# A two-block model on one core: the order of the first stage's sums, tables, folds and slabs

## The chip, the core and the metric

The kernel runs on one core of a Trainium2 chip. All work is float32. The metric is the device time of one execution in microseconds; the profile adds one profiled execution, with the time of every instruction. Engines: TensorE (PE; its weight loads are PEld), VectorE (DVE), ScalarE (ACT), GpSimd (POOL), and SyncE (SP), which here only issues transfers.

## What is computed

A token model with 512 tokens of width 1024 (`x`) and 256 context tokens (`ctx`), in two blocks of two layers each. The change touches only the beginning of the first layer of the first block:

```python
def adaln_params(cvec, w, b):
    return jnp.split(jax.nn.silu(cvec) @ w + b, 6, axis=-1)

def fourier_mix(h, w_o, b_o):
    bsz, t, _ = h.shape
    hg = h.astype(jnp.float32).reshape(bsz, t, FNET_GROUPS, FNET_GROUP_DIM)
    f = jnp.fft.fft2(hg, axes=(1, 3), norm='ortho').real
    return f.reshape(bsz, t, D_MODEL).astype(h.dtype) @ w_o + b_o

# layer 0 of first_block
sh1x, sc1x, g1x, sh2x, sc2x, g2x = adaln_params(c, ada_w[i], ada_b[i])
hx = rmsnorm(x, norm_g[i, 0]) * (1.0 + sc1x) + sh1x
x = x + g1x * fourier_mix(hx, fnet_wo[fi], fnet_bo[fi])      # the same for ctx with c_ctx
hx = rmsnorm(x, norm_g[i, 1]) * (1.0 + sc2x) + sh2x
x = x + g2x * ec_moe(hx, moe_router[i], moe_wg[i], moe_wu[i], moe_wd[i])
```

Then follow a second layer with a recurrent mixer and another expert stage, and a second block of two attention layers with feed-forward parts. None of that is touched.

## The kernel before

Everything is laid out with channels on the 128 partitions: `resx` is x as 8 tiles (KT = 8) of 128 x 512, `resc` the context as 8 tiles of 128 x 256. Weights come as slabs of 128 x 4096 float32 (2 MB), one transfer each, into a ring of three places; slab n goes to place n modulo 3, in the order of the list `FRONT`: a0 to a3, w0, w1, a4 to a11, tables. The slabs a0 to a11 are `ada_w` of the layer, w0 and w1 are the output weights of the Fourier mixer, and "tables" holds cosines and sines that are fetched in two pieces into `work` (`load_tables`: first C and S, 514 columns, later the other 2690). `vecs` are all small vectors, `tabs1` constant matrices of 2338 columns whose first 128 are the identity `ident` and whose next 128 are `ones`.

There is no scheduler. Each engine's program is written out by hand in the order in which it runs, and semaphores join them. An engine waits in its own order, so whatever stands behind a waiting instruction waits too. `Steps` and `Side` only count semaphore values. SP issues transfers in order as well, each behind its own wait: slab n may be loaded when slab n - 3 has been used, which PE reports (`slab_used`) for the a slabs, and GpSimd (`norm_pool`) for w0 and w1.

The front, in order:

- **Sums of squares.** ACT computes silu(c) into `cs`, changes its function table, and squares the 8 tiles of x into `sqx0`. DVE squares the context (`sqc0`), adds its halves (step "context"), then adds the halves of x's squares (steps "added"). PE sums over the partitions by multiplying with `ones`: first the context, then x (step "sums"). ACT makes 1/root of it (`rstd`).
- **Folding of tokens.** DVE multiplies x and the context by `rstd` (`ux`, `uc`) and adds and subtracts mirrored tokens into `hx` and `hc` (step "folded"), since a cosine needs only the even part and a sine the odd part.
- **Modulation 0.** PE multiplies silu(c) with a0 to a3 (`ada_slab`), ACT copies the sums, PE transposes them with `ident` (`ada_turned(0)`) and then runs some matmuls whose results nobody reads (`kept_warm`). DVE makes scale and shift of them (`modulation(0)`).
- **Scaling.** ACT scales and shifts the 8 tiles of `hx` (L2247, L2248), two instructions a tile; DVE does the same for the 8 tiles of `hc` (L2846, L2847), and counts each in `norm_dve`.
- **First phase** (channels): PE multiplies `hx` and `hc` with C and S, twice 7 tiles, the seventh being the two Nyquist columns `nyq`. DVE copies each result out of PSUM (L2856). PE uses six banks and waits for a copy before it uses a bank again.
- **GpSimd's folds.** Behind step "folded" GpSimd adds and subtracts the halves of w0 and of w1 into `wsum` (L3696, L3697, four instructions of 128 x 2048), and copies 4 rows of the tables (L3700). The third phase reads `wsum`.
- **Second phase** (tokens): PE multiplies with the cosines and sines of tokens, 9 results, copied by DVE (L2865, L2867). Before them DVE clears a small table (memset, L2859).
- **Modulation 1**: a4 to a7, copy, transposes. ACT then adds a bias to resx and resc, PE makes a shift for the router.
- **Third phase** (output weights): for f = 0 to 7, two results each; ahead of f = 0 to 3 stand a8 to a11. DVE adds the results to resx and resc.
- **Routing and experts.** PE, DVE and ACT choose tokens for 16 experts; GpSimd gathers the rows of the first two with indirect transfers (`gathered`). PE runs `kept_warm(P[1], 8)` before it transposes them and goes through 96 expert slabs.

Of the kernel before, what the change touches and what calls it, by code (L numbers as in the profile page):

```python
# [29 lines left out]
KT = D // 128  # L30
NX, NC = 512, 256
# [29 lines left out]
TAB1 = {}  # L61
# [6 lines left out]
NTAB1 = _n  # L68
# [12 lines left out]
FN = {}  # L81
# [212 lines left out]
AD_DVE = [("context",)] + [("added", _k) for _k in range(4)] + [("folded",)] + [("mod", _g) for _g in range(3)]  # L294
# [111 lines left out]
def build(nc, slabs_d, vecs_d, tabs1_d, tabs2_d, aux_d, lora_d, x_d, ctx_d, out_d, kv_d):  # L406
# [5 lines left out]
    with stack:  # L412
# [3 lines left out]
        def sem(name):  # L416
            return stack.enter_context(nc.semaphore(name))
# [31 lines left out]
        ad_pe, ad_dve, ad_act, x_loaded, context_loaded, waves_loaded = (sem(n) for n in ("ad_pe", "ad_dve", "ad_act", "x_loaded", "context_loaded", "waves_loaded"))  # L449
        rt_pe, rt_dve, rt_act, places_loaded = (sem(n) for n in ("rt_pe", "rt_dve", "rt_act", "places_loaded"))  # L450
# [49 lines left out]
        adarow = [work[:, at:at + HALF] for at in (KT * HALF, KT * HALF + HALF, 2 * KT * HALF - HALF)]  # L500
        cs = cut(work, WORK - 2 * KT - KT * 32, KT, 32)
# [368 lines left out]
        def _(sp):  # L870
            sp.dma_start(resx[:, :, :], x_d.rearrange("(k p) t -> p k t", p=128)).then_inc(x_loaded, 16)
            sp.dma_start(vecs[:, :], vecs_d).then_inc(tables_loaded, 16)
            sp.dma_start(resc[:, :, :], ctx_d.rearrange("(k p) t -> p k t", p=128)).then_inc(context_loaded, 16)
            sp.dma_start(tabs1[:, :], tabs1_d[:, 0:NTAB1]).then_inc(tables_loaded, 16)
# [4 lines left out]

            load_tables(0, FN["S"][1])  # L880
# [54 lines left out]
            used = 0  # L935
            for n in range(RING, f0):
                before = FRONT[n - RING]
                if before in ("w0", "w1"):
                    sp.wait_ge(norm_pool, 1 + int(before[1]))
                else:  # L940
                    used += 1
                    sp.wait_ge(slab_used, used)
                if FRONT[n] == "tables":
                    sp.dma_start(ring[n % RING][:, 0, 0:4], slabs_d[n][:, 0:4]).then_inc(slab_loaded[n % RING], 16)
                else:
                    load(n)
                if FRONT[n] == "a3":
                    load_tables(FN["S"][1], FN["w128"][1])
# [68 lines left out]
        def _(pe):  # L1017
# [79 lines left out]
            pe.wait_ge(tables_loaded, 32)  # L1097
# [40 lines left out]

            pe.wait_ge(*ad_done("dve", "context"))
            for k in range(4):  # L1140
                mm(P[5][:, 0:NC], ones, sqc0[:, k, :], k, 4)
            for k in range(4):
                pe.wait_ge(*ad_done("dve", "added", k))
                m = mm(P[4][:, :], ones, sqx0[:, k, :], k, 4)
# [4 lines left out]
            pe.wait_ge(fed, me.next("fed"))  # L1149
            for n in range(4):  # L1150
                ada_slab(n)
            ada_turned(0)
            kept_warm(P[0], 4)
# [10 lines left out]
            for pair in range(2):  # L1164
                for i, (src, at, n, part, _) in enumerate(FN_TILES):
                    if me.reuses():

                        pe.wait_ge(drained, me.reused())
                    b = me.next_bank()
                    name, wide_ = ("S", 128) if part is AO else ("C", 129)  # L1170
                    for q in range(2):
                        for k in range(2):
                            kt = 4 * pair + 2 * q + k
                            if i == 0:
                                shifted(kt)
                            if i == 4:
                                scaled(kt)
                            m = mm(b[0:n, wide_ * q:wide_ * (q + 1)], src[:, kt, at:at + n], fn(name, k, wide_), k, 2)
                    m.then_inc(filled, me.add("filled"))
            pe.wait_ge(fed, me.next("fed"))  # L1180
# [27 lines left out]
            me.t["slab"].n += 2  # L1208
            for n in range(4, 8):
                ada_slab(n)  # L1210
# [57 lines left out]
            def first_routing():  # L1268
# [57 lines left out]
                kept_warm(P[1], 8)  # L1326
# [860 lines left out]
        def _(act):  # L2187
# [35 lines left out]
            act.wait_ge(tables_loaded, 32)  # L2223
# [10 lines left out]

            act.wait_ge(x_loaded, 16)
            for k in range(4):
                for half in range(2):
                    tile_square(k + 4 * half, [(resx, sqx0)], wait=False)
            act.wait_ge(*ad_done("pe", "sums"))
# [515 lines left out]
        def _(v):  # L2755
# [41 lines left out]
            v.memset(tiny, 1e-6)  # L2797
            v.drain().then_inc(fed, me.add("fed"))
            t["answered"].n += 1
            ad = Steps(AD_DVE)  # L2800
            v.wait_ge(context_loaded, 16)
# [3 lines left out]
            for k in range(4):  # L2805
                v.wait_ge(norm_act, 2 * k + 2)
                v.tensor_tensor(sqx0[:, k, :], sqx0[:, k, :], sqx0[:, k + 4, :], ALU.add).then_inc(ad_dve, ad.one("added", k))
# [15 lines left out]
            def modulation(g):  # L2823

                v.wait_ge(*ad_done("pe", "turned", g))
                v.wait_ge(tables_loaded, 32)
# [628 lines left out]
            with me.loop("layer", 2) as l:  # L3455
# [91 lines left out]
                v.wait_ge(tables_loaded, 48)  # L3547
# [140 lines left out]
        def _(pool):  # L3688
            me = Side(pool, K)
            pool.wait_ge(norm_act, KT + 1)  # L3690
            pool.wait_ge(*ad_done("dve", "folded"))
# [401 lines left out]
```

## Time and profile before

| what | value |
|---|---|
| median of three runs | 3798.23 us (3795.86 to 3805.44) |
| the profiled execution | 3813.2 us, its span 3811.4 us |
| mean granted TensorE clock | 0.987 of full |
| PE busy over the span | 3615.1 us, 95% |
| first phase, copies included | about 45 to 75.5 us of the span |
| second phase | 75.5 to 92 us |
| third phase | 110.7 to 170 us |
| routing | 171 to 215 us |
| first expert stage | 215 to 800 us |

Times in the rows count from the start of the span. A matmul of float32 stands in the trace as two records, so 32 records of 128 x 129 are 16 matmuls; a slab of `ada_w` is 32 matmuls and 64 records. A timeline row merges neighbours of a kind, with their count (x) and the time from the first one's start to the last one's end. The brackets give the idle time of the engine before the row and what ended it. An engine that is not the bound may idle without harm; what counts is PE's idle time.

### The profile page before, as it was taken

The page shows a single profiled execution, that of the slowest core. Times are in us where ns is not written, and L with a number is a line of the kernel's source. Part 1 is how long each engine was busy: PE and PEld are TensorE (multiplying, and loading weights), DVE is VectorE, ACT ScalarE, POOL GpSimd, SP SyncE. Part 2 cuts the span into 40 slices and gives each one's busy share as a digit, 9 for nine tenths or more (in the row PEclk, how much of TensorE's full clock was granted, in tenths as well). Part 3 has the DMA queues.
Part 4 walks back from the last instruction along what each step waited for, and adds up shares of the span by engine and source line. Part 5 has one row for each costly group of instructions (what it writes and reads, how often), then busy time and mean ns, then how long its engine had stood idle before and what let it go on. Part 6 is the DMA issues. An engine that isn't in the chain of part 4 may idle for free.

```text
span 3811.4 us, 84045 instructions
## 1 busy us (share of the span) xinstructions
PE 3615.1 (95%) x35378; PEld 2256.1 (59%) x35378; DVE 1599.2 (42%) x3423; ACT 802.1 (21%) x1802; POOL 704.3 (18%) x634
## 2 busy tenths in 40 slices
PE   6999999989989899899999999989999999999998
PEld 4544444455567777764444344455888744658887
DVE  5321111164566666643212133742445437425454
ACT  1210010020145565541000011070000010610000
POOL 2100001000044444420000000002343300023433
PEclk8999999999999999999999999999999999999999
DMA  6699999942200000022999981101222211012221
GB/s 267 266 394 383 383 378 374 390 189 86 92 12 14 18 18 13 14 82 113 427 429 428 428 338 45 67 24 64 83 78 86 98 45 67 24 48 86 88 89 45
DMA packets 56774, 626.04 MB, mean 164 GB/s; under 512 B 6080, under 2 KB 9408, under 8 KB 20928
## 3 DMA queue, kind: packets, MB, share of 16 engines
q1 hardware_dynamic: 50096, 599.22, 39.2%
q0 software_dynamic: 3968, 14.16, 1.3%
q10 hardware_dynamic: 2448, 8.91, 0.6%
q8 instruction: 195, 3.19, 0.3%
q14 instruction: 67, 0.55, 0.0%
HBM read 604.18 MB, written 18.09 MB: 163 GB/s over the span
## 4 chain that ended last, share of the span: by engine, by line
PE 85%; DVE 6%; DMA 3%; issue 2%; ACT 2%; DVEq 1%; ACTq 1%; PEld 0%; PEldq 0%; SPq 0%
PE bank L1022 69%; PE bank L1588 11%; DMA work<-slabs 2%; PE bank L1970 1%; PE bank L1983 1%; PE bank L1643 1%; PE bank L1050 1%; DVE hx L2788 1%; DVE work L2764 1%; ACT work L2667 1%; ACTq L2668 1%; DMA ring<-slabs 1%; PEld bank L1022 0%; DVE work L2773 0%; PE bank L1451 0%
## 5 line engine op out<-in xcount | busy, mean ns | idle before, releaser
L1022 PE MATMUL bank<-work 128*64 128x512 f32 (+11 forms) x5232 | 874.8, 424 | 29.6 <-DVE work L2856 13.9
L1022 PEld LDWEIGHTS bank<-work 128*128 128x128 f32 (+6 forms) x5232 | 504.4, 153 | 369.2 <-issue 273.6
L1022 PE MATMUL bank<-ring,work 128*32 128x256 f32 (+2 forms) x4416 | 472.2, 429 | 21.8 <-DMA ring<-slabs 14.2
L1022 PE MATMUL bank<-hx,ring 128*128 128x512 f32 (+1 forms) x1344 | 483.3, 514 | 5.1 <-DVE hx L2788 2.8
L1022 PE MATMUL bank<-work,ring 128*128 128x256 f32 (+1 forms) x1616 | 479.7, 455 | 6.5 <-DVE work L3150 3.4
L1022 PEld LDWEIGHTS bank<-work,ring 128*128 128x128 f32 x1616 | 306.2, 190 | 173.5 <-issue 131.7
L1022 PEld LDWEIGHTS bank<-hx,ring 128*128 128x128 f32 x1344 | 254.3, 191 | 222.0 <-issue 200.7
L1022 PEld LDWEIGHTS bank<-ring,work 128*32 128x32 f32 (+1 forms) x4416 | 193.0, 122 | 287.0 <-issue 242.8
L3835 POOL TENSOR_TENSOR work<-ring 128x512 f32<-128x512 f32 (+1 forms) x44 | 69.4, 1577 | 1564.5 <-ACT work L2196 1167.4
L2764 DVE TENSOR_TENSOR work<-work,bank 128x256 f32<-128x256 f32 x240 | 91.8, 416 | 384.6 <-ACT work L2742 380.3
L1588 PE MATMUL bank<-work 64*64 64x64 f32 x9216 | 196.8, 228 | 28.3 <-issue 17.0
L1022 PE MATMUL bank<-hx,work 128*32 128x256 f32 (+3 forms) x1344 | 211.4, 416 | 1.1 <-issue 1.0
L1588 PEld LDWEIGHTS bank<-work 64*64 64x64 f32 x9216 | 177.8, 139 | 39.2 <-issue 37.3
L1022 PEld LDWEIGHTS bank<-hx,work 128*32 128x32 f32 (+2 forms) x1344 | 131.9, 145 | 63.1 <-issue 40.2
L2742 ACT ACTIVATE work<-bank 128x256 f32<-128x256 f32 x48 | 18.5, 385 | 693.8 <-PE bank L1022 693.8
L1588 PE MATMUL bank<-ring,work 64*64 64x128 f32 (+2 forms) x2912 | 152.5, 287 | 5.8 <-DVE hx L3260 3.1
L3053 DVE TENSOR_TENSOR work<-work,bank 128x256 f32<-128x256 f32 x16 | 6.8, 423 | 325.7 <-PE bank L1022 325.7
L3640 DVE SCALAR_TENSOR_TENSOR work<-work 128x256 f32<-128x256 f32 x176 | 122.9, 713 | 15.5 <-issue 6.0
L1022 PE MATMUL bank<-resc,work 128*128 128x256 f32 x512 | 121.2, 379 | 0.6 <-DVE resc L3628 0.6
L1588 PEld LDWEIGHTS bank<-ring,work 64*64 64x64 f32 x2912 | 106.5, 133 | 15.2 <-issue 14.1
L3054 DVE TENSOR_TENSOR work<-work,bank 128x512 f32<-128x512 f32 x32 | 21.9, 685 | 208.3 <-PE bank L1022 208.3
L3188 DVE TENSOR_TENSOR work<-bank,tabs_sb 128x384 f32<-128x384 f32 x160 | 87.9, 555 | 44.3 <-PE bank L1588 41.9
(391 smaller groups left out, 4538.0 us busy)
## 6 DMA issues: line engine op xcount, KB each, us to landing
ring<-slabs SPq DMA_DIRECT2D x176, 2048.0 KB, 10.6
work<-slabs SPq DMA_DIRECT2D x82, 2048.0 KB, 15.9
hx<-slabs SPq DMA_DIRECT2D x17, 2048.0 KB, 12.0
work<-kv SPq DMA_DIRECT2D x18, 384.0 KB, 3.1
kv<-work SPq DMA_DIRECT2D x2, 3072.0 KB, 15.9
kv<-work ACTq DMA_DIRECT2D x6, 512.0 KB, 5.3
resx<-xT SPq DMA_DIRECT2D x1, 2048.0 KB, 8.4
kv<-work POOLq DMA_DIRECT2D x1, 2048.0 KB, 29.6
```

The lines of the kernel that those rows point to most:

```text
L1022: return pe.matmul(out, lhsT, rhs, start=(k == 0), stop=(k == n - 1))
L1050: pe.matmul(b[:, 0:width], ident, tabs1[:, 0:width], start=True, stop=True)
L1588: m = pe.matmul(out[other if across else r], lhsT[r], rhs[r], start=first, stop=last)
L1643: pe.matmul(outw[:, 0:n], wa2[two[d], 0:128], HW[two[d], at:at + n], start=True, stop=True)
L1970: m = pe.matmul(out[:, 0:n], q[rows_of(h), 128 * i:128 * i + 128], key[rows_of(h), k0:k1], start=(part == 0), stop=(part == parts - 1 and ...
L1983: m = pe.transpose(out[:, a:a + 128], S[:, h, a:a + 128], ident)
L2667: act.activation(S[:, h, 0:n], at_bank("L", u, h)[:, 0:n], ACT.Exp, bias=low, scale=-1.0, accum_out=sums[u % 2][:, h:h + 1])
L2668: act.drain().then_inc(at_act, ak.one("exp", u, h))
L2764: v.tensor_tensor(out, a, b, op)
L3188: v.tensor_tensor(by_halves(TL, g), level_banks("H", g), bc(levels[:, 1 - d, l, :].unsqueeze(1).unsqueeze(1), 128, 2, 3, CH), ALU.mult).th ...
L3640: return v.scalar_tensor_tensor(dst, x, 1.0, y, ALU.mult, ALU.subtract)
L3835: pool.tensor_tensor(s3, a["a11"], a["a21"], ALU.subtract).then_inc(ff_pool, 1)
```

## The change

1. SP fetches only the first 128 columns of `tabs1` (the identity) ahead of a0. The other 2210 columns and the rest of the sine tables are issued behind a3, the first piece of the sine tables behind a2. `vecs`, the identity and the rest of tabs1 get semaphores of their own. PE waits for the identity before the transposes, and for the rest of tabs1 before `kept_warm`; `modulation` on DVE waits for vecs and for the rest of tabs1.
2. ACT loads its silu table at once, squares x as soon as x has landed, and computes silu(c) behind the squares. DVE adds the halves of x's squares first and squares the context behind them. PE sums x first and the context second, with a block of ones that DVE has written itself (`early_ones`), so that it doesn't wait for tabs1.
3. GpSimd's folds wait for the eighth count of `norm_dve`, which is DVE's last scaling of the context, in place of step "folded".
4. PE takes slab a4 between the first and the second phase; a5 to a7 stay behind the second.
5. `kept_warm` runs 3 matmuls for 4 behind the transposes, and 5 for 8 before the experts.

```diff
-AD_DVE = [("context",)] + [("added", _k) for _k in range(4)] + [("folded",)] + [("mod", _g) for _g in range(3)]
+AD_DVE = [("added", _k) for _k in range(4)] + [("context",), ("folded",)] + [("mod", _g) for _g in range(3)]
...
+        early_ones = adarow[2][:, 0:128]
...
-            sp.dma_start(vecs[:, :], vecs_d).then_inc(tables_loaded, 16)
+            sp.dma_start(vecs[:, :], vecs_d).then_inc(vectors_loaded, 16)
             sp.dma_start(resc[:, :, :], ctx_d.rearrange("(k p) t -> p k t", p=128)).then_inc(context_loaded, 16)
-            sp.dma_start(tabs1[:, :], tabs1_d[:, 0:NTAB1]).then_inc(tables_loaded, 16)
+            first = TAB1["ident"][1]
+            sp.dma_start(tabs1[:, 0:first], tabs1_d[:, 0:first]).then_inc(identity_loaded, 16)
...
-            load_tables(0, FN["S"][1])
...
+            load_tables(0, FN["S"][1])
             for n in range(RING, f0):
...
                 if FRONT[n] == "a3":
+                    sp.dma_start(tabs1[:, first:NTAB1], tabs1_d[:, first:NTAB1]).then_inc(tables_loaded, 16)
                     load_tables(FN["S"][1], FN["w128"][1])
...
-            pe.wait_ge(tables_loaded, 32)
...
+            pe.wait_ge(fed, me.next("fed"))
+            for k in range(4):
+                pe.wait_ge(*ad_done("dve", "added", k))
+                mm(P[4][:, :], early_ones, sqx0[:, k, :], k, 4)
             pe.wait_ge(*ad_done("dve", "context"))
             for k in range(4):
-                mm(P[5][:, 0:NC], ones, sqc0[:, k, :], k, 4)
-            for k in range(4):
-                pe.wait_ge(*ad_done("dve", "added", k))
-                m = mm(P[4][:, :], ones, sqx0[:, k, :], k, 4)
+                m = mm(P[5][:, 0:NC], early_ones, sqc0[:, k, :], k, 4)
...
             for n in range(4):
                 ada_slab(n)
+            pe.wait_ge(identity_loaded, 16)
             ada_turned(0)
-            kept_warm(P[0], 4)
+            pe.wait_ge(tables_loaded, 16)
+            kept_warm(P[0], 3)
...
+            me.t["slab"].n += 2
+            ada_slab(4)
             pe.wait_ge(fed, me.next("fed"))
             pe.wait_ge(waves_loaded, 32)
...
-            me.t["slab"].n += 2
-            for n in range(4, 8):
+            for n in range(5, 8):
                 ada_slab(n)
...
-                kept_warm(P[1], 8)
+                kept_warm(P[1], 5)
...
+            act.preload_act_table_set("silu_and_others")
+            act.wait_ge(x_loaded, 16)
+            for k in range(4):
+                for half in range(2):
+                    tile_square(k + 4 * half, [(resx, sqx0)], wait=False)
+            act.wait_ge(vectors_loaded, 16)
             act.wait_ge(fed, 1)
...
             v.memset(tiny, 1e-6)
+            v.memset(early_ones, 1.0)
...
-                v.wait_ge(tables_loaded, 32)
+                v.wait_ge(vectors_loaded, 16)
+                v.wait_ge(tables_loaded, 16)
...
             pool.wait_ge(norm_act, KT + 1)
-            pool.wait_ge(*ad_done("dve", "folded"))
+            pool.wait_ge(norm_dve, KT)
```

Where the instructions stand. PE at the end of the first phase, before (`work 2x129` are the Nyquist columns, `work 128x257` the first result of the second phase):

```order
L1022 MATMUL bank<-work,hc 127x128 x4
L1022 MATMUL bank<-work 2x129 x4
L1022 MATMUL bank<-work 128x257 x3
L1022 MATMUL bank<-work 128x129 x2
L1022 MATMUL bank<-work 128x255 x2
L1022 MATMUL bank<-work 128x127
```

and now:

```order
L1025 MATMUL bank<-work,hc 127x128 x4
L1025 MATMUL bank<-work 2x129 x4
L1025 MATMUL bank<-ring,work 32x128 x32
L1025 MATMUL bank<-work 128x257 x3
L1025 MATMUL bank<-work 128x129 x2
L1025 MATMUL bank<-work 128x255 x2
L1025 MATMUL bank<-work 128x127
```

The 32 matmuls out of the ring, slab a4, have moved between the phases; behind the second one 96 are left of 128.

SP at the program's start, before (`tabs_sb` is tabs1, `work<-slabs` the sine tables):

```order
L871 DMA resx<-xT 128x8x512
L872 DMA vecs_sb<-vecs 128x607
L873 DMA resc<-ctxT 128x8x256
L874 DMA tabs_sb<-tabs 128x2338
L878 DMA work<-slabs 128x514
L884 DMA ring<-slabs 128x4096 x4
L878 DMA work<-slabs 128x2690
L884 DMA ring<-slabs 128x4096 x10
```

and now:

```order
L873 DMA resx<-xT 128x8x512
L874 DMA vecs_sb<-vecs 128x607
L875 DMA resc<-ctxT 128x8x256
L877 DMA tabs_sb<-tabs 128x128
L885 DMA ring<-slabs 128x4096 x3
L881 DMA work<-slabs 128x514
L885 DMA ring<-slabs 128x4096
L950 DMA tabs_sb<-tabs 128x2210
L881 DMA work<-slabs 128x2690
L885 DMA ring<-slabs 128x4096 x10
```

Most of tabs1 has moved behind a3, and stands ahead of w0 like the rest of the sine tables.

GpSimd's folds, with the semaphores that each waits for, before:

```order
L3696 TENSOR_TENSOR work<-ring 128x2048 [waits slab_loaded1,ad_dve,norm_act]
L3697 TENSOR_TENSOR work<-ring 128x2048
L3696 TENSOR_TENSOR work<-ring 128x2048 [waits slab_loaded2]
L3697 TENSOR_TENSOR work<-ring 128x2048
L3700 COPY work<-work 4x1024 [waits waves_loaded]
```

and now:

```order
L3704 TENSOR_TENSOR work<-ring 128x2048 [waits slab_loaded1,norm_dve,norm_act]
L3705 TENSOR_TENSOR work<-ring 128x2048
L3704 TENSOR_TENSOR work<-ring 128x2048 [waits slab_loaded2]
L3705 TENSOR_TENSOR work<-ring 128x2048
L3708 COPY work<-work 4x1024 [waits waves_loaded]
```

The order is the same; the first fold's wait for a step of DVE (`ad_dve`) has become one for DVE's scaling (`norm_dve`).

## Rows read from the trace of the kernel before

**Rows 1.** The page's first line, the whole program.

```profile
span 3811.4 us, 84045 instructions
```

**Rows 2.** Windows: length, busy us (instructions) by engine, PE clock, DMA share, GB/s.

```profile
core 0: us, PE busy (x) PEld busy (x) DVE busy (x) ACT busy (x) POOL busy (x), PEclk, DMA share, GB/s
0.00:45.00 45.00, 22.23 (x283) 15.73 (x284) 22.57 (x30) 11.35 (x20) 0.20 (x4) 0.89 0.96 392
45.00:75.00 30.00, 15.66 (x114) 13.28 (x113) 25.34 (x25) 5.43 (x13) 19.37 (x5) 0.77 0.64 253
75.00:110.00 35.00, 27.95 (x402) 20.91 (x406) 6.49 (x15) 2.44 (x5) 0.00 (x0) 0.95 0.43 176
215.00:800.00 585.00, 581.32 (x5234) 246.17 (x5236) 91.62 (x225) 56.68 (x146) 39.41 (x54) 1.00 0.94 369
...
31.00:42.00 11.00, 7.65 (x130) 6.30 (x131) 9.36 (x9) 0.60 (x1) 0.00 (x0) 0.53 1.01 426
```

**Rows 3.** Timeline, 37 to 50 us: start, us, engine, line, operation, [idle <-releaser].

```profile
37.28 3.64 PE L1022 MATMUL bank<-ring,work 128*32 128x128 f32 x64 [1.09 <-DMA ring<-slabs]
...
42.25 3.60 PE L1050 MATMUL bank<-tabs_sb 128*128 128x512 f32 x8
42.45 0.19 DVE L2764 TENSOR_TENSOR mod<-bank,vecs_sb 128x32 f32<-128x32 f32 x1 [2.02 <-PE bank L1117]
...
46.92 3.16 PE L1022 MATMUL bank<-work,hx 128*128 128x129 f32 x26 [0.40 <-ACT hx L2248]
```

**Rows 4.** DMA issues of the first 8 us: KB each, median us to landing.

```profile
tabs_sb<-tabs SPq DMA_DIRECT2D x1, 1169.0 KB, 13.4
```

**Rows 5.** Timeline, the first phase, 44 to 75 us.

```profile
44.05 0.35 DVE L2846 TENSOR_SCALAR hc<-hc,work,mod 128x128 f32<-128x128 f32 x1
...
44.50 0.34 DVE L2846 TENSOR_SCALAR hc<-hc,work,mod 128x128 f32<-128x128 f32 x1
...
45.55 4.67 POOL L3696 TENSOR_TENSOR work<-ring 128x2048 f32<-128x2048 f32 x1 [45.08 <-DMA ring<-slabs]
45.66 4.64 DVE L2847 TENSOR_SCALAR hc<-hc,work 128x127 f32<-128x127 f32 x1
...
65.29 2.07 DVE L2856 COPY work<-bank 128x258 f32<-128x258 f32 x6
...
65.75 1.88 PE L1022 MATMUL bank<-work 128*2 128x129 f32 x8 [13.89 <-DVE work L2856]
...
67.56 4.63 PE L1022 MATMUL bank<-work,hx 128*128 128x129 f32 x32
...
73.90 1.05 PE L1022 MATMUL bank<-work 128*2 128x129 f32 x8
```

**Rows 6.** Timeline, 1082 to 1083.6 us, in the second layer: DVE beside GpSimd.

```profile
1082.30 0.64 POOL L3802 TENSOR_TENSOR work<-work,tabs_sb 128x256 f32<-128x256 f32 x1 [19.61 <-ACT work L2396]
...
1082.77 0.41 DVE L3260 COPY hx<-bank 128x256 f32<-128x256 f32 x1
```

**Rows 7.** Timeline, PE from 75 to 119 us.

```profile
75.54 16.50 PE L1022 MATMUL bank<-work 2*128 2x257 f32 x73 [0.60 <-DVEq L2857]
...
102.90 3.24 PE L1022 MATMUL bank<-ring,work 128*32 128x128 f32 x64 [4.86 <-DMA ring<-slabs]
...
108.57 0.31 PE L1022 MATMUL bank<-ring,work 128*32 128x128 f32 x3
...
117.06 1.96 PE L1022 MATMUL bank<-ring,work 128*32 128x128 f32 x64
```

**Rows 8.** DMA issues at 54.8 us (a5), 64.1 (a6) and 94.0 (a7).

```profile
ring<-slabs SPq DMA_DIRECT2D x1, 2048.0 KB, 7.6
...
ring<-slabs SPq DMA_DIRECT2D x1, 2048.0 KB, 8.4
...
ring<-slabs SPq DMA_DIRECT2D x1, 2048.0 KB, 8.9
```

**Rows 9.** Timeline, 206 to 215 us: PE's warming matmuls, SP behind `gathered`.

```profile
206.76 10.02 PE L1050 MATMUL bank<-tabs_sb 128*128 128x512 f32 x16
...
214.38 0.33 SPq L894 DMA_DIRECT2D hx<-slabs  x1
```

More of the change, by code:

```diff
@@ L449, in build @@
         ad_pe, ad_dve, ad_act, x_loaded, context_loaded, waves_loaded = (sem(n) for n in ("ad_pe", "ad_dve", "ad_act", "x_loaded", "context_loaded", "waves_loaded"))
+        vectors_loaded, identity_loaded = sem("vectors_loaded"), sem("identity_loaded")
         rt_pe, rt_dve, rt_act, places_loaded = (sem(n) for n in ("rt_pe", "rt_dve", "rt_act", "places_loaded"))
@@ L1148, in _ @@
             pe.wait_ge(answered, 1)
-            pe.wait_ge(fed, me.next("fed"))
             for n in range(4):
                 ada_slab(n)
+            pe.wait_ge(identity_loaded, 16)
             ada_turned(0)
-            kept_warm(P[0], 4)
+            pe.wait_ge(tables_loaded, 16)
+            kept_warm(P[0], 3)
             me.first_bank()
@@ L2222, in _, with ada_copied @@
             both = [(resx, sqx), (resc, sqc)]
-            act.wait_ge(tables_loaded, 32)
+            ad = Steps(AD_ACT)
+            def ada_copied(g):
+                act.wait_ge(*ad_done("pe", "summed", g))
+                act.activation(adarow[g], P[7][:, :], ACT.Copy).then_inc(ad_act, ad.one("copied", g))
+            act.preload_act_table_set("silu_and_others")
[4 more added lines that the diff above has]
+            act.wait_ge(vectors_loaded, 16)
             act.wait_ge(fed, 1)
@@ L2227, in _ @@
             act.preload_act_table_set("natural_log_exp_and_others")
-            ad = Steps(AD_ACT)
-            def ada_copied(g):
-                act.wait_ge(*ad_done("pe", "summed", g))
-                act.activation(adarow[g], P[7][:, :], ACT.Copy).then_inc(ad_act, ad.one("copied", g))
[L2235 to L2238, printed above, removed]
             act.wait_ge(*ad_done("pe", "sums"))
@@ L2800, in _ @@
             ad = Steps(AD_DVE)
+            for k in range(4):
+                v.wait_ge(norm_act, 2 * k + 2)
+                v.tensor_tensor(sqx0[:, k, :], sqx0[:, k, :], sqx0[:, k + 4, :], ALU.add).then_inc(ad_dve, ad.one("added", k))
             v.wait_ge(context_loaded, 16)
@@ L2804, in _ @@
             v.tensor_tensor(sqc0[:, 0:4, :], sqc0[:, 0:4, :], sqc0[:, 4:8, :], ALU.add).then_inc(ad_dve, ad.one("context"))
-            for k in range(4):
-                v.wait_ge(norm_act, 2 * k + 2)
-                v.tensor_tensor(sqx0[:, k, :], sqx0[:, k, :], sqx0[:, k + 4, :], ALU.add).then_inc(ad_dve, ad.one("added", k))
             v.wait_ge(norm_act, KT + 1)
@@ L3546, in _ @@
                 scaled(segs, rstd2, lambda k, j: pv[:, k:k + 1])
-                v.wait_ge(tables_loaded, 48)
+                v.wait_ge(tables_loaded, 32)
                 taken("cqi0", ("x", "cqi0"))
```

## The prediction

> **What bounds the kernel now.** I read the page first: one core, span 3811.4 us [rows 1]. Everything that the diff moves lies before 217 us. The table of windows [rows 2] says where TensorE (PE) is not the bound: it is busy 22.2 of the first 45 us, 15.7 of the 30 us from 45 to 75, 28.0 of the 35 from 75 to 110, but 581.3 of the 585 us of the expert stage. So time can be won in the first 110 us, and what is won there should stay won, because PE, not a transfer, fills what follows.
>
> The timeline then names the wait that ends last in each piece. To 41 us it is the stream of transfers: slab a3 starts on PE at 37.28, when it has landed, and takes 3.64 us, about twice the 1.96 of a slab at full clock [rows 3, 7]. Behind it come its copy, the transposes, VectorE's (DVE) `mod(0)` at 42.45 and ScalarE's scaling; PE goes on in earnest at 46.92, released by ScalarE's fourth tile [rows 3]. The worst piece is 45 to 66 us [rows 5]: GpSimd starts to fold w0 at 45.55, in instructions of 4.67 us, and DVE's context scaling, whose pairs had started 0.45 us apart, now has instructions of 4.64. Only behind the sixteenth, at 65.29, do DVE's copies out of PSUM (L2856) start, and PE has waited 13.89 us for the first. The last piece is a7: its ring place is free only when a4 is used, which stands behind the second phase, and PE waits 4.86 us more at 102.90 [rows 7].
>
> **Step 1, tables fetched later.** tabs1 is 1169 KB ahead of a0 [rows 4]; 64 KB of it (the identity) stay. The 1105 KB that leave are 1.13 MB: at 392 to 426 GB/s [rows 2] that is 2.9 to 2.7 us. a3 lands 2.7 us sooner, as long as it is issued (after a0 is used) before the stream runs dry, which step 2 makes safer. Its consumers follow: `mod(0)` at 39.8, ScalarE's fourth tile at 44.2 for 46.92. The rest of tabs1 is now behind a3 and lands 2.7 us after it, at about 37.3; `mod(0)` and the warming matmuls, which now wait for it, are reached at 39.5 or later, so 2 us cover that wait; without them both would start late by what is missing. w0 and a4 stand behind the same bytes as before. **Gain 2.7.**
>
> **Step 2, squares when x lands, sums of x before those of context.** The sums end several us sooner. But PE then waits for a1, a2 and a3 as before, and DVE's products only end earlier ahead of a `mod(0)` that they did not delay: DVE had been idle for 2.02 us before it, waiting for PE's transposes [rows 3]. Worth 0, hidden by a3's landing; it would cost only if a0 were used later than today.
>
> **Step 3, three warming matmuls for four (L1050).** Four end at 45.85 under the wait for 46.92 [rows 3]; three end at about 42.3 under 44.2. Worth 0, unless the clock falls in the 2 us behind them (below).
>
> **Step 4, GpSimd behind DVE's scaling.** With `mod(0)` at 39.8, scaling starts near 41 and its eight pairs at 0.45 us end at 44.6. w0 lands at 45.4 as now, so GpSimd starts at the same 45.5 and ends its four folds (4.6 us each) at the same 64.1: its chain costs nothing new. DVE goes on to the PSUM copies. The price hangs on one question: does a copy out of PSUM also stand still under a GpSimd instruction? The nearest rows are at 1082 us [rows 6]: a 128x256 copy out of PSUM starts 0.47 us into a GpSimd tensor_tensor of 0.64 us and takes 0.41 us. So I take no blocking. The 13.89 us go, and with them the half clock that the gap brought: the 8 Nyquist records took 1.88 us behind it and 1.05 later, and the 32 records behind them 4.63 where 26 at full clock took 3.16 [rows 3, 5]; that is 0.8 + 0.7. The first phase ends at 73.90 + 1.05 - 2.7 - 13.9 - 1.5 = 56.8. **Gain 15.4.** Late next is nothing on DVE: its memset (L2859) may stand under GpSimd for up to 4.6 us, but PE has six banks free there, over 10 us of work.
> The Trainium skill, SBUF — State Buffer, sections "SBUF: two separate sides" and "Who interferes with whom", says that VectorE and GpSimd take a common port pair exclusively, for a whole instruction, and lists copies among VectorE's that do; taken alone it puts L2856 under the lock (the third rival). VectorE: DVE Perf Modes, section "Mode 2×_2P", restricts the two-port form to SBUF operands; by that L2856 is free. The scaling under GpSimd (4.64 us) agrees with the first, the copy at 1082.77 (0.41 us) with the second.
>
> **Step 5, slab a4 between the phases.** From w0's 45.4, a4 lands two slabs of 2.1 MB later, 4.9 us each at 426 GB/s, at 55.2. At 56.8 PE takes it without a wait: 1.96 us and 0.1 to hand over [rows 7]. It covers the 0.6 us in which PE waited for DVE's last copy. The second phase starts at 58.9 for 75.54 and, taking 16.5, ends at 75.4. SP's loads stand in order: a5 behind GpSimd's first fold, a6 behind the second, a7 behind a6. a6 takes 8.4 us from 64.1 [rows 8], a7 one slab more: 77.4. PE reaches a7 at 75.4 + 2 x 2.05 = 79.5 and ends it at 81.5, for 102.90 + 3.24 = 106.14 now. So here 24.6 us are won: 2.7, 15.4, 0.6 and, of a7, the wait of 4.86 and 1.3 of half clock, less roundings.
> The new wait is a8. It is loaded when a5 is used, now at 77.5; a load alone takes 7.6 to 8.9 us [rows 8], so it lands at 85.1 to 86.4. PE is there at 84.0 (2.43 us behind a7's end, as 108.57 is now [rows 7]). Cost 1.1 to 2.4, I take 1.8. If the clock is then at half, a8 takes 3.6 for 1.96: of 0 to 1.7 I take 0.5. **Net 22.3** at the third phase's start. a9 to a11 have over 6 us of PE work between them, and the stream needs 4.9 a slab.
>
> **Step 6, five warming matmuls for eight ahead of the experts.** Eight (16 records) took 10.02 us from 206.76 [rows 9]; at full clock, where 8 records take 3.60 [rows 3], they take 7.2, so some six or seven ran at half. The gathered rows were there at 214.4, where SP's wait for them ends [rows 9], yet PE was in matmuls until 216.8. Five would have ended near 214.3, and at full clock eight end at 214.0 and nothing is won. So 0 to 2.3; I take 1.2.
>
> **Sum.** 22.3 + 1.2 = 23.5 us. The profiled execution took 3813.2 (span 3811.4), so a like one would take 3789.7; the median of the three runs is 15 us under it, and 3798.2 - 23.5 = 3774.7, 0.62% less. About 0.3% (11.4 us) is what a measurement of this kernel tells from no change; its three runs spread over 9.6.
>
> **Rivals.**
> *The clock or small waits eat part.* The front still has idle pieces (behind a1, up to 44.2, before a8), and the granted clock was 0.53 from 31 to 42 and 0.77 from 45 to 75 [rows 2]. If one more stretch of 10 us of PE work runs at half, the gain is 13.5: 3784.7. For it: less warming. Against: after the long gap PE was back at full clock within some 4 us of work.
> *Nothing arrives, because the expert stage ends on its transfers.* They are busy 0.94 there. Against: PE is busy 0.994, and the loads hang on steps that all move. It would give about 3796.
> *The copies stand under GpSimd after all* (the change does not do what it says). Then one gets through per GpSimd instruction until 65.3, 9 of 14 remain, the first phase ends near 70 (gain 5), and a4's new place still removes the wait for a7, less a8's: 10 to 11 us, 3787.5. Against it: [rows 6].
> *Slower.* With three warming matmuls and sparse work from 42.3 to 44.2 the clock falls to half as PE enters the first phase and stays there through both: 12.8 + 16.5 = 29 us of work doubled against 23.5 won, 3803.7. It decides from 23.5 us of work at half. Against: the clock was 0.95 from 75 to 110 with PE busy 28 of 35 us [rows 2].
>
> **How the numbers follow.** Forecast 0.70; clock or small waits 0.13; copies blocked 0.06; nothing arrives 0.07; slower 0.04. Range: at best 24.6 - 1.1 + 2.3 = 25.8, and 3.4 more if a2 and a3 ran at full clock, gives 3769; with the runs' spread 3767. Upwards it takes in the first and third rival, 3788. Faster by over 0.3%: 0.70 + 0.13 + a part of copies blocked, less a little for the spread, 0.84; within 0.3%: 0.12; slower: 0.04.
>
> **What would show it.** Right: DVE's 16 scalings at about 0.3 us each and over before GpSimd starts; copies (L2856's) of 0.43 us under its 4.6; the wait of 13.9 gone; a4 at 57 without a wait; a new wait of 1 to 2.5 us for a8 near 84; the third phase 22 us sooner, the expert stage 22 to 25. Wrong: copies of over 1 us under GpSimd; `mod(0)` waiting for the tables near 40; a granted clock of one half in either phase; an expert stage longer than its 585 us.

## The result

| | before | the changed kernel |
|---|---|---|
| median of the runs of one measurement | 3813.61 us (3795.86 to 3819.13, 11 runs) | 3791.74 us (3787.61 to 3794.96, 11 runs) |
| ratio | | 0.995, 95% interval 0.9936 to 0.9964 |
| profiled execution, its span | 3813.2, 3811.4 us | 3789.2, 3787.4 us |

The change is faster by 13.7 to 24.4 us. The two profiled executions differ by 24.0 us, and the prediction's sum of gains was 23.5; the match is closer than it earned, since 2.6 us of the 24.0 arise in a part that nothing changed (below). Yet the predicted time, 3774.7 with a range of 3767 to 3788, lies 17 us under the measured one, which is outside the range. The sum was taken off the median of three runs, 3798.2; more runs of the same kernel give 3813.6. Why the median of three runs of the kernel before could lie 15 us under that of eleven is the main thing that the experiments had to settle.

### The profile page after: what moved, and what is told of

Its sections match the earlier page's. It is cut to its first block, busy times and chain, and to the rows that moved or that the text cites. A ratio compares the mean times of both kernels' runs of the same rounds, so it can differ in the third digit from the quotient of the medians.

```text
span 3787.4 us, 84032 instructions
## 1 busy us (share of the span) xinstructions
PE 3608.6 (95%) x35370; PEld 2250.7 (59%) x35370; DVE 1582.7 (42%) x3424; ACT 802.6 (21%) x1802; POOL 703.2 (19%) x634
## 4 chain that ended last, share of the span: by engine, by line
PE 84%; DVE 5%; DMA 3%; issue 2%; ACT 2%; DVEq 1%; PEld 1%; ACTq 1%; PEldq 0%; POOL 0%; POOLq 0%; SPq 0%
PE bank L1025 68%; PE bank L1593 12%; DMA work<-slabs 2%; PE bank L1975 1%; PE bank L1988 1%; PE bank L1648 1%; PEld bank L1025 1%; DVE hx L2794 1%; DMA ring<-slabs 1%; DVE work L2770 0%; ACT work L2673 0%; ACTq L2674 0%; DVE work L2779 0%; DVE work L3217 0%; PE bank L1456 0%
## 5 line engine op out<-in xcount | busy, mean ns | idle before, releaser
L1025 PE MATMUL bank<-work 128*32 128x256 f32 (+11 forms) x5248 | 882.3, 425 | 27.6 <-DVE work L2810 11.2
L1025 PEld LDWEIGHTS bank<-work 128*128 128x128 f32 (+4 forms) x5248 | 508.3, 153 | 370.6 <-issue 287.2
L3648 DVE SCALAR_TENSOR_TENSOR work<-work 128x256 f32<-128x256 f32 x176 | 123.4, 716 | 15.4 <-issue 6.1
## 6 DMA issues: line engine op xcount, KB each, us to landing
work<-slabs SPq DMA_DIRECT2D x82, 2048.0 KB, 15.7
kv<-work SPq DMA_DIRECT2D x2, 3072.0 KB, 15.7
```

What stands on the lines that cost most here:

```text
L1025: return pe.matmul(out, lhsT, rhs, start=(k == 0), stop=(k == n - 1))
L3648: return v.scalar_tensor_tensor(dst, x, 1.0, y, ALU.mult, ALU.subtract)
```

## The profile after

The page's first line, answering [rows 1]:

```profile
span 3787.4 us, 84032 instructions
```

The windows of the changed kernel (length, busy us and instructions by engine, PE clock, DMA share, GB/s), answering [rows 2]:

```profile
31.00:42.00 11.00, 8.26 (x110) 5.87 (x103) 6.34 (x17) 1.91 (x4) 0.00 (x0) 0.65 1.01 425
45.00:75.00 30.00, 29.72 (x240) 23.18 (x238) 10.81 (x23) 2.91 (x7) 19.04 (x5) 1.00 0.80 316
45.00:90.00 45.00, 41.03 (x519) 32.69 (x518) 11.96 (x28) 9.91 (x21) 19.04 (x5) 0.96 0.81 321
200.00:800.00 600.00, 591.24 (x5427) 253.94 (x5424) 105.22 (x251) 67.44 (x163) 39.42 (x54) 0.99 0.94 370
```

From 45 to 75 us PE is now busy for 29.7 of the 30 us, where before it had been busy for 15.7 of them [rows 2]. To 42 us the granted clock is still low, 0.65.

The timeline of the changed kernel, 34 to 60 us (start, us, engine, line, operation, in brackets the idle time before it and what ended it), answering [rows 3] and [rows 5]:

```profile
34.83 3.64 PE L1025 MATMUL bank<-ring,work 128*32 128x128 f32 x64 [1.94 <-DMA ring<-slabs]
...
39.94 0.19 DVE L2770 TENSOR_TENSOR mod<-bank,vecs_sb 128x32 f32<-128x32 f32 x1 [4.25 <-PE bank L1119]
...
44.49 0.28 DVE L2855 TENSOR_SCALAR hc<-hc,work 128x127 f32<-128x127 f32 x1
...
45.73 4.53 POOL L3704 TENSOR_TENSOR work<-ring 128x2048 f32<-128x2048 f32 x1 [45.26 <-DMA ring<-slabs]
45.82 0.43 DVE L2864 COPY work<-bank 128x258 f32<-128x258 f32 x1 [0.47 <-PE bank L1025]
...
54.92 4.53 POOL L3704 TENSOR_TENSOR work<-ring 128x2048 f32<-128x2048 f32 x1 [0.18 <-issue]
...
56.59 1.99 PE L1025 MATMUL bank<-ring,work 128*32 128x128 f32 x61
...
57.58 0.48 DVE L2867 MEMSET work<- 128x512 f32 x1 [0.29 <-issue]
...
58.87 16.50 PE L1025 MATMUL bank<-work 2*128 2x257 f32 x73 [0.28 <-issue]
```

Slab a3 starts 2.45 us sooner and still takes 3.64 us. DVE's last context scaling ends at 44.77 (44.49 + 0.28), 1.0 us ahead of GpSimd's first fold, and the fold was released by w0's landing, not by DVE: its new wait costs nothing. The copies out of PSUM (L2864) take 0.43 us while a fold of 4.53 runs, and so does the memset: 0.48 us at 57.58, inside the fold that ends at 59.45 (54.92 + 4.53). The wait of 13.89 us is gone, a4 follows the first phase without a wait, and the second phase starts at 58.87 for 75.54 [rows 7].

The same view further on, answering [rows 7] and [rows 9]: the new wait for a8, the third phase, and the stretch ahead of the experts.

```profile
86.10 3.39 PE L1025 MATMUL bank<-ring,work 128*32 128x128 f32 x64 [1.89 <-DMA ring<-slabs]
...
89.58 6.58 PE L1025 MATMUL bank<-work 128*128 128x386 f32 x18
...
184.73 6.57 PE L1053 MATMUL bank<-tabs_sb 128*128 128x512 f32 x10
192.14 1.09 PE L1400 MATMUL bank<-tabs_sb,work 128*128 128x128 f32 x8 [0.84 <-DMA work<-kv,index]
...
196.47 19.09 PE L1025 MATMUL bank<-ring,work 128*64 128x512 f32 x144 [2.58 <-ACT work L2329]
215.37 5.50 PE L1025 MATMUL bank<-hx,work 128*32 128x256 f32 x48
```

And the kernel before at the same three points:

```profile
110.66 6.47 PE L1022 MATMUL bank<-work 128*128 128x386 f32 x18
...
216.62 1.04 PE L1395 MATMUL bank<-tabs_sb,work 128*128 128x128 f32 x8
...
220.88 16.13 PE L1022 MATMUL bank<-ring,work 128*64 128x512 f32 x144 [2.58 <-ACT work L2323]
236.82 5.49 PE L1022 MATMUL bank<-hx,work 128*32 128x256 f32 x48
```

The distance between the two is 21.1 us at the third phase, 24.5 at the transposes of the gathered tokens (216.62 to 192.14), and 21.45 behind the first 144 expert records (236.82 to 215.37), since these now take 19.09 for 16.13 us. The other 2.6 us of the 24.0 arise later, where nothing was changed. That part, from the start of the experts' next stage (215.37 and 236.82) to the end of the span, takes 3567.0 to 3575.7 us over the thirteen profiled executions of this study (3574.6 before, 3572.0 in the changed kernel), so 2.6 us of it are scatter.

## The experiments

The ratios are to the kernel before, which ran on the same chip beside them; its runs are told of in a paragraph of their own below. Steps are numbered as in the prediction.

**fold_early: step 4 undone, all else kept.**

```
-            pool.wait_ge(norm_dve, KT)
+            pool.wait_ge(*ad_done("dve", "folded"))
```

> The changed kernel with one line of it undone: GpSimd's folds wait for step folded again, not for VectorE's context scaling. Theory A (tables and fold are each enough): with tabs1 behind a3 the sixteen scalings end at 44.8 us of the span and w0 lands at 45.3, so the fold starts at 45.7 whatever it waits for, the scalings stay at 0.3 us, and the time is that of the changed kernel within 2 us. Theory B (the prediction's step 4, the fold's new wait brings the 13.9 us): scalings of 4.6 us under the fold, VectorE's PSUM copies from 65 us, 14 to 18 us slower than the changed kernel.

Measured: 3788.86 us (3782.34 to 3794.69, 10 runs), ratio 0.9949 (0.9935 to 0.9964). Its timeline has the last scaling at 44.63 and the fold at 45.87:

```profile
44.63 0.28 DVE L2855 TENSOR_SCALAR hc<-hc,work 128x127 f32<-128x127 f32 x1
...
45.87 4.53 POOL L3704 TENSOR_TENSOR work<-ring 128x2048 f32<-128x2048 f32 x1 [45.41 <-DMA ring<-slabs]
```

GpSimd was allowed to go first and did not, because w0 had not landed. With the tables out of the way, the new wait is not needed: the prediction gave it the whole credit for the 13.9 us.

**tables_first: step 1 undone, step 4 kept** (the rest of tabs1 is issued right behind the identity).

```
             sp.dma_start(tabs1[:, 0:first], tabs1_d[:, 0:first]).then_inc(identity_loaded, 16)
+            sp.dma_start(tabs1[:, first:NTAB1], tabs1_d[:, first:NTAB1]).then_inc(tables_loaded, 16)
...
-                    sp.dma_start(tabs1[:, first:NTAB1], tabs1_d[:, first:NTAB1]).then_inc(tables_loaded, 16)
```

> The changed kernel with all of tabs1 fetched ahead of a0 again (identity and rest right behind each other); the fold's new wait stays. Theory A and B alike: mod(0) 2.6 us later, near 42.5, scalings near 43.6 to 47.2 at 0.3 us each, GpSimd's first fold at 47.3 in place of 45.7, second phase 2.6 us later than the changed kernel's 58.87, the whole 2 to 3 us slower than the changed kernel. If the tables were worth nothing: 0.

Measured: 3793.43 us (3786.76 to 3800.56, 12 runs), ratio 0.9965 (0.9947 to 0.9982). Now GpSimd does wait for DVE, and no scaling is stretched:

```profile
46.90 0.29 DVE L2855 TENSOR_SCALAR hc<-hc,work 128x127 f32<-128x127 f32 x1
...
47.33 4.54 POOL L3704 TENSOR_TENSOR work<-ring 128x2048 f32<-128x2048 f32 x1 [46.87 <-DVE hc L2855]
...
91.94 6.89 PE L1025 MATMUL bank<-work 128*128 128x386 f32 x18
```

The third phase starts 2.4 us later than in the changed kernel, which is the price of the tables at that point. Steps 1 and 4 each remove the stall without the other.

**both_back: both undone** (the two edits above together).

> The changed kernel with both of these undone: all of tabs1 ahead of a0, and GpSimd's folds behind step folded. Theory A: w0 lands at 45.4 with only four pairs scaled, the port block is back, scalings of 4.6 us until 65.3, a PE wait of 13 to 14 us for the first PSUM copy, second phase at 77 for 58.87 and the whole 17 to 19 us slower than the changed kernel. Rival (the order of squares and sums gave part of the gain): less than 15.

Measured: 3806.76 us (3785.94 to 3815.44, 12 runs), ratio 0.9996 (0.9979 to 1.0012). Two runs took 3785.94 and 3794.14, the ten others 3802.39 to 3815.44. The profiled execution is the fastest of them, and shows no stall:

```profile
37.34 1.95 PE L1025 MATMUL bank<-ring,work 128*32 128x128 f32 x64 [1.90 <-DMA ring<-slabs]
...
40.77 0.19 DVE L2770 TENSOR_TENSOR mod<-bank,vecs_sb 128x32 f32<-128x32 f32 x1 [5.05 <-PE bank L1119]
...
45.32 0.28 DVE L2855 TENSOR_SCALAR hc<-hc,work 128x127 f32<-128x127 f32 x1
...
45.59 4.54 POOL L3704 TENSOR_TENSOR work<-ring 128x2048 f32<-128x2048 f32 x1 [45.12 <-DMA ring<-slabs]
```

This was the experiment that changed the theory. If its two groups of times are the stall and its absence, the same kernel runs with the stall and without it: it is a **race**, in which either DVE's last scaling or GpSimd's first fold comes first. Here a3 ran at full clock (1.95 us), the sixteen scalings end at 45.60, and GpSimd, released by w0's landing, starts at 45.59, just too late to stretch one. If a3 takes 3.64, `mod(0)` comes at 42.4 [rows 3] and the scalings, undisturbed, need until 47.2 (46.90 + 0.29 in fold_only below, where a3 takes 3.64 too), so GpSimd gets in between. The next two runs force the race either way.

**both_back_warm: the race decided by the clock.** In both_back, PE is kept busy with spare matmuls while it waits for a2 and a3:

```
             for n in range(4):
+                for _ in range((0, 0, 4, 2)[n]):
+                    pe.matmul(P[0][:, :], early_ones, resx[:, 0, :], start=True, stop=True)
                 ada_slab(n)
```

> The kernel with tabs1 first and the folds behind step folded (runs from 3786 to 3815), plus 4 matmuls without use ahead of a2 and 2 ahead of a3, where PE waits for transfers. Theory R with the clock as what decides: a3 then runs at full clock (1.96 us for 3.64), mod(0) comes at 40.8 for 42.4, the scaling ends at 45.6 as the fold starts, and wins or loses one instruction of 4.6 us: median 3788 to 3795, few runs above 3800. Rival (the clock has nothing to do with it): the same two clusters, median near 3807.

Measured: 3791.38 us (3787.59 to 3793.37, 6 runs), ratio 0.9954 (0.994 to 0.9967). All six are as fast as the changed kernel, and none is in the group above 3802. The window from 31 to 42 us has a granted clock of 1.00 (that is 2.4 GHz), where it was 0.53 before [rows 2]:

```profile
31.00:42.00 11.00, 9.44 (x144) 5.69 (x143) 5.46 (x11) 0.86 (x2) 0.00 (x0) 1.00 1.00 423
```

and in the timeline a3 takes 1.95 us (start 37.56), the last scaling starts at 45.53 and ends at 45.82, and GpSimd's fold starts at 45.83. The margin is as thin as in both_back; a run that loses it by a little would have one scaling stretched, and none of the six times shows even that.

**late_scaling: the race forced the other way.** In fold_early, DVE's loop of scalings waits for w0 as well:

```
             tt(nyq, nyq, mod[:, 0, 0, :, :], ALU.add)
+            v.wait_ge(slab_loaded[1], 32)
             for k in range(KT):
```

> The changed kernel with the race forced to be lost: GpSimd's folds wait for step folded, and VectorE begins its context scaling only when w0 has landed (45.3 us for 41.1). Theory R: scaling and fold start together, the scalings stand under the four folds, one or two between two of them free, and end near 66 to 68 us; PE waits 18 to 22 us for the first PSUM copy, which then is no longer than 0.43 us; the whole 17 to 22 us slower than the changed kernel in every run, near 3810, in one cluster of no more than 15 us. Rival: the later start alone costs its 4 us and no more.

Measured: 3811.89 us (3805.68 to 3816.74, 12 runs), ratio 1.0006 (0.9993 to 1.0019). All twelve are in the group above 3802, 21.6 us above the changed kernel on the same chip. The timeline:

```profile
45.70 0.35 DVE L2855 TENSOR_SCALAR hc<-hc,work,mod 128x128 f32<-128x128 f32 x1 [3.98 <-DMA ring<-slabs]
45.84 4.58 POOL L3705 TENSOR_TENSOR work<-ring 128x2048 f32<-128x2048 f32 x1 [45.38 <-ACT hx L2254]
45.96 4.55 DVE L2856 TENSOR_SCALAR hc<-hc,work 128x127 f32<-128x127 f32 x1
...
50.43 4.53 DVE L2855 TENSOR_SCALAR hc<-hc,work,mod 128x128 f32<-128x128 f32 x1
...
54.88 0.28 DVE L2856 TENSOR_SCALAR hc<-hc,work 128x127 f32<-128x127 f32 x1
...
55.08 4.56 DVE L2855 TENSOR_SCALAR hc<-hc,work,mod 128x128 f32<-128x128 f32 x1
...
59.56 4.53 DVE L2856 TENSOR_SCALAR hc<-hc,work 128x127 f32<-128x127 f32 x1
64.01 0.33 DVE L2855 TENSOR_SCALAR hc<-hc,work,mod 128x128 f32<-128x128 f32 x1
...
79.19 16.50 PE L1025 MATMUL bank<-work 2*128 2x257 f32 x73 [0.28 <-issue]
```

Each of the four folds stretches one scaling to its own length, and a short one slips through where GpSimd changes slabs (54.88) and at its end (64.01). With fifteen scalings left instead of the seven of the kernel before, DVE still needs until 67 us; the second phase starts 20.3 us later than in the changed kernel. Of this, up to 4.6 us are the later start itself (45.70 for 41.08), the rest is the stretching. What counts is neither GpSimd's wait nor the tables by themselves, but whether the scalings are over before the folds begin.

**The runs of the kernel before** agree with the race. On three chips it ran 32, 17 and 17 times. Each time the sorted times have a hole: 3797.0 to 3802.8, 3800.8 to 3805.6, and 3798.2 to 3806.8 us. Below it lie 6, 5 and 3 runs, above it 26, 12 and 14; the medians are 3811.6, 3809.1 and 3810.9. On the second chip the hole is no proof by itself, since a gap of 5.0 us stands below it too (3794.6 to 3799.6). Of the three runs that stood ahead of the prediction two, 3795.86 and 3798.23, are from below the hole, while the third, 3805.44, and the profiled execution, 3813.2, are from above.

**fold_only: step 4 alone in the kernel before** (GpSimd waits for `norm_dve`).

```
-            pool.wait_ge(*ad_done("dve", "folded"))
+            pool.wait_ge(norm_dve, KT)
```

> The kernel before with one line changed: GpSimd's folds wait for VectorE's last context scaling. Theory R (in the kernel before the scaling races with w0's landing at 45.4 us; mostly it loses and waits up to 19 us under the folds, sometimes it wins, and its runs fall in two clusters for that reason): this kernel always wins, so its runs stand together near the kernel before's fast ones, 3792 to 3801, none above 3803; median about 3796; in the profile the fold starts near 47.3, scalings at 0.3 us, no PE wait of 13.9. Rival S (the kernel before's spread has another cause): runs still spread over more than 20 us, in two clusters.

Measured: 3798.92 us (3792.6 to 3803.55, 11 runs), ratio 0.9978 (0.9966 to 0.999). One group of 11 us, with no run above 3804. Five of its runs, 3800.98 to 3803.55, lie in the hole of the kernel before on this chip, and its median is 3 us over the 3796 that was expected. Its timeline:

```profile
46.90 0.29 DVE L2847 TENSOR_SCALAR hc<-hc,work 128x127 f32<-128x127 f32 x1
...
47.33 4.54 POOL L3696 TENSOR_TENSOR work<-ring 128x2048 f32<-128x2048 f32 x1 [46.87 <-DVE hc L2847]
...
87.22 3.64 PE L1022 MATMUL bank<-ring,work 128*32 128x128 f32 x64 [4.86 <-DMA ring<-slabs]
...
97.57 2.69 PE L1022 MATMUL bank<-work 128*128 128x386 f32 x5
```

a7 starts 15.7 us sooner than in [rows 7], as the prediction's 15.4 had it. The wait of 4.86 us for a7 is unchanged, and with a7 and a8 at half clock (3.64 and 3.65 us) the third phase is 13.1 us sooner. (The view ends at 100 us, inside its last row.)

**a4_behind: step 5 undone** (a4 behind the second phase again).

```
-            me.t["slab"].n += 2
-            ada_slab(4)
...
-            for n in range(5, 8):
+            me.t["slab"].n += 2
+            for n in range(4, 8):
                 ada_slab(n)
```

> The changed kernel with slab a4 behind the second phase again. The wait for a7 comes back (about 5 us near 80), the wait of 1.9 us for a8 goes: third phase 2 to 4 us later than 89.6, the whole 2 to 4 us slower than the changed kernel. If a4's place were worth the 6.1 us that the prediction gave it before a8's wait: 6 us.

Measured: 3795.69 us, the median of seven runs: six from 3787.15 to 3799.27, and one of 5040.65, far from every other run, which is left out of the ratio, 0.996 (0.9946 to 0.9974). Its timeline:

```profile
85.39 3.64 PE L1025 MATMUL bank<-ring,work 128*32 128x128 f32 x64 [4.90 <-DMA ring<-slabs]
...
92.00 3.27 PE L1025 MATMUL bank<-ring,work 128*32 128x128 f32 x61
...
95.40 4.86 PE L1025 MATMUL bank<-work 128*128 128x386 f32 x13
```

The third phase starts 5.8 us later than in the changed kernel, where 2 to 4 were expected. (This view too ends at 100 us.) The ratio puts the total some 4 us later, which the intervals don't tell from nothing; the timeline does. The place is worth more than the wait: 4.9 less 1.9 for a8 gives 3.0, and most of the rest is clock, since here a7 ran at half as well, 3.64 us, against only a8 in the changed kernel.

**warm8: step 6 undone**, `kept_warm(P[1], 8)` for `kept_warm(P[1], 5)`.

> The changed kernel with eight warming matmuls ahead of the experts in place of five. In the changed kernel five ended at 191.3, the rows were there at 192.1, and the first 72 matmuls of the experts then took 19.1 us (16.1 before) as the granted clock was at half from 195.6 to 202.5. Theory A (the five let the clock fall): warming ends near 194, the first 72 matmuls take 16.1, and the whole is 0.5 to 1.5 us faster than the changed kernel. Rival (the fall is chance and has nothing to do with them): 1.5 to 2.5 us slower, or the stretch at 19.1 again.

Measured: 3790.61 us (3786.78 to 3796.44, 11 runs), ratio 0.9951 (0.9937 to 0.9965). Its timeline:

```profile
184.90 9.70 PE L1053 MATMUL bank<-tabs_sb 128*128 128x512 f32 x16
194.44 1.04 PE L1400 MATMUL bank<-tabs_sb,work 128*128 128x128 f32 x8
...
198.70 16.13 PE L1025 MATMUL bank<-ring,work 128*64 128x512 f32 x144 [2.59 <-ACT work L2329]
214.64 5.50 PE L1025 MATMUL bank<-hx,work 128*32 128x256 f32 x48
```

With five, the transposes start 2.3 us sooner, and the first 144 expert records take 19.09 us for 16.13: the granted clock is at half from 195.6 to 202.5 us, and with eight it is full there. The two fronts are not alike, though: a3 ran at full clock in this execution (1.96 us), and the third phase started at 88.29 for 89.58. From there to the experts' next stage eight take 126.4 us (to 214.64) and five 125.8 (to 215.37). Nor is the pair typical. Over all profiled executions this stretch takes 124.5 to 127.9 us with five (eight executions) and 123.9 to 128.0 with eight (five executions), and the 144 records take 17.55 to 19.09 us with five, and with eight 16.13 twice, but also 17.66, 17.82 and 18.77. What five or eight are worth is not shown, in the timeline or in the total.

**three_more: the changed kernel with three more edits**: the spare matmuls of both_back_warm ahead of a2 and a3, a5 taken inside the second phase, and eight warming matmuls.

```
                         mm(b[:, 255:382], AO[0:127, 2, 128 * g:128 * g + 128], fn("sc")[0:127, :], 0, 1).then_inc(filled, me.add("filled"))
+                        if g == 1:
+                            ada_slab(5)
...
-            for n in range(5, 8):
+            for n in range(6, 8):
                 ada_slab(n)
```

> The changed kernel with three more edits: the useless matmuls ahead of a2 and a3, slab a5 taken inside the second phase so that a8 is loaded sooner, and eight warming matmuls ahead of the experts. Expected: a3 at 1.96 us (gain 1.7), no wait of 1.9 us for a8 and a8 at full clock (gain 3.3), experts' first matmuls in 16.1 us (gain 0.7): third phase near 84.6 for 89.6, the whole 5 to 6 us under the changed kernel, about 3786. If the clock takes it back elsewhere: no difference.

Measured: 3783.05 us (3779.52 to 3790.41, 6 runs), ratio 0.9939 (0.9924 to 0.9954). Its timeline:

```profile
34.86 1.95 PE L1025 MATMUL bank<-ring,work 128*32 128x128 f32 x64 [1.37 <-DMA ring<-slabs]
...
64.82 1.95 PE L1025 MATMUL bank<-ring,work 128*32 128x128 f32 x64
...
82.61 1.91 PE L1025 MATMUL bank<-ring,work 128*32 128x128 f32 x61
...
84.66 6.47 PE L1025 MATMUL bank<-work 128*128 128x386 f32 x18
```

a3 runs at full clock, a8 has no wait and no half clock, since a5 gives up its ring place some 10 us sooner, and the third phase starts 4.9 us sooner than in the changed kernel.

**after_again and three_more_again: the two side by side on one chip**, unchanged.

> The changed kernel once more, beside the next one on one chip: 3788 to 3795 as before, ratio to the kernel before 0.994 to 0.996.

> The changed kernel with the matmuls without use ahead of a2 and a3, slab a5 inside the second phase and eight warming matmuls, once more, beside the changed kernel on one chip: third phase 5 us sooner, the whole 5 to 8 us under the changed kernel; if the earlier 3783 was the chip and not the edits, less than 3.

Measured: 3790.31 us (3786.32 to 3794.18, 6 runs), ratio 0.9947 (0.9931 to 0.9964), and 3784.37 us (3780.38 to 3788.95, 6 runs), ratio 0.9933 (0.9916 to 0.9949). The timeline of three_more_again:

```profile
82.80 3.36 PE L1025 MATMUL bank<-ring,work 128*32 128x128 f32 x64
...
86.24 6.61 PE L1025 MATMUL bank<-work 128*128 128x386 f32 x18
```

The second kernel is 5.9 us faster by the medians, though their runs overlap by 2.6 us. Of this its third phase shows 3.0 us (86.24 for 89.24 in after_again), where 5 were expected: a8 again has no wait, but this time it ran at half clock. By the medians it is the fastest kernel of this study.

## Why the prediction was wrong, point by point

**The step that failed is the sum.** "3798.2 - 23.5 = 3774.7" takes the stall away from a median that mostly did not have it. Every duration was read from the profiled execution of 3813.2, so the gain belongs to that, and the line before it had it: "a like one would take 3789.7", 2.0 us under the measured median. The text noted that the median was 15 us under the profile and did not ask what that was. By the experiments it was the race: the wait of 13.9 us that the change removes was missing from two of the three runs, as far as their times tell, for none of them was profiled. A median of more runs, 3813.6, would have given 3790.1. The range failed with it: but for 2 us of the runs' spread at its lower end its terms were bounds of costs, and none was a doubt of the base.

That 23.5 and 24.0 agree so well is in part luck. At the third phase the gain was 21.1 for 22.3, at the experts' next stage 21.45, and the rest is scatter of the unchanged part.

**What bounds the kernel**: right as a reading of one execution. That this was one of two courses was not seen, though the rows had the sign: the pairs of scalings, 0.45 us apart, would have ended at 47.2, and GpSimd started at 45.55 [rows 5], less than 2 us before.

Three kernels split the 21.1 us at the third phase: from before to fold_only 13.1 (110.66 to 97.57), from there to tables_first 5.6 (91.94), and to the changed kernel 2.4 (89.58).

- **Step 1 (2.7 forecast)**: 2.4 at the third phase, and a3 starts 2.6 us sooner than in tables_first (34.83 for 37.46); right. That it decides the race by itself was missed.
- **Steps 2 and 3 (0)**: nothing in any trace speaks against it; neither was run alone.
- **Step 4 (15.4)**: 15.7 at a7 in fold_only; 2.6 of it is lost again before the third phase, 2.1 of that by the half clock of a7 and a8 (3.64 and 3.65 us for 3.24 and 1.96). Its price question was answered as forecast, copies out of PSUM are free under GpSimd, and the memset, feared for up to 4.6 us, is free too. The credit was wrong: once the tables are moved, fold_early is as fast without this step.
- **Step 5**: the milestones held to 0.1 us (second phase 58.9 forecast, 58.87; a7's end 81.5, 81.4), and the wait for a8 was 1.89 for 1.8. The term that was mis-sized is a8's half clock, 0.5 forecast and 1.4 measured (3.39 for 1.96 us); the net was 21.1 for 22.3.
- **Step 6 (1.2 of 0 to 2.3)**: from the third phase to the experts' next stage the changed kernel takes 125.8 us, the kernel before 126.2 and warm8 126.4, a gain of 0.4 to 0.6 that is smaller than the scatter of the other executions. Its size stays open.
- **The rivals.** Copies under GpSimd: out. Nothing arrives, because the expert stage ends on transfers: out, the 21 us stay. Slower by the clock in both phases: out, it was 1.00 from 45 to 75 us and 0.96 to 90. Clock and small waits eating part: in small, 1.4 at a8 and, in this execution, about 3 in the experts' first records.

The Trainium skill, SBUF — State Buffer, section "Who interferes with whom", says that copies and `tensor_scalar` can take the port pair that VectorE shares with GpSimd where their operands meet the conditions of the two-port mode, and that an instruction with at most one SBUF input outside that mode does not contend. The trace agrees: the scalings stand still (4.55 us under a fold of 4.58), the copies out of PSUM (0.43) and the memset (0.48) do not. The prediction's "taken alone it puts L2856 under the lock" left out that condition.

**What stays open.** In the ten profiled executions without spare matmuls a3 took 1.95 and 1.96 us in two (both_back and warm8), 2.98 and 3.31 in two (tables_first and after_again) and 3.64 in six. Why was not found: the changed kernel and after_again are one program, and warm8 differs from them only far behind a3. With the spare matmuls it took 1.95 or 1.96 in all three. No run of the kernel before from below the hole was profiled, and none of both_back from above it: that the stall is what divides them rests on fold_only, both_back_warm and late_scaling. The spread of the runs above the hole, 3802 to 3820, is not accounted for either; how many scalings are left and the 8.7 us of scatter in the unchanged part may both enter.

## What to carry to other kernels

When a profiled execution and the median of a few runs differ by more than the runs of a settled program do, ask what differs before a gain is taken off either: a gain read in one execution belongs to that execution's time. Before two timelines are compared at a late point, subtract what they differ by at an earlier one, as the two counts of warming matmuls show. Where a stall needs one engine to start before another has ended, look how close the two are (here 0 to 2 us) and what each start hangs on, since the stall may be there in some runs only; forcing the order both ways, as both_back_warm and late_scaling do, shows its price at once. Folding and scaling beside each other on GpSimd and VectorE cost up to 20 us here, while copies out of PSUM beside the same folds cost nothing.

## What was not expected of the hardware

- The clock of TensorE decided an order between two other engines: both_back, with a3 at full clock, 1.95 us, showed no stall, and with spare matmuls that keep a3 there none of its six runs is above 3802. The kernel before, with a3 at 3.64, waited for 13.9 us.
- Six spare matmuls whose result nothing reads, in time in which PE was waiting for slabs anyway, brought the window from 31 to 42 us to a granted clock of 1.00; without them it was 0.50 to 0.91. They cost nothing that the timeline shows, and a3 was 1.7 us shorter than in the changed kernel.
- With five warming matmuls ahead of the experts the 144 records behind them never ran wholly at full clock (17.55 to 19.09 us in eight executions); with eight they did in two of five (16.13).
